# Shifting every on-chip buffer: activation tiles from 64 to 96 bytes past a 128-byte boundary

## What is computed

```python
# first block
proj = rmsnorm(x) @ w_in                       # 2048 x 6176
x = x + concat(attention, gated_linear_attention) @ w_out
h = rmsnorm(x)
x = x + (silu(h @ w_gate) * (h @ w_up)) @ w_down          # hidden width 5632
# second block
h = rms_norm(x) * (1 + sc1) + sh1              # shifts and scales from c @ w_ada
x = x + g1 * (concat(retention, rwkv, moba)(h @ w_in_2) @ w_out_2)
h = rms_norm(x) * (1 + sc2) + sh2
u = h @ w_ffn_up                               # 2048 x 11264, then a conv of width 3
x = x + g2 * ((silu(gate) * val) @ w_ffn_down)
return rms_norm(x)
```

## Time and profile before

| | us |
|---|---|
| median of 3 runs | 2443.33 |
| lowest and highest | 2442.01, 2447.37 |
| the profiled execution, span from first to last instruction | 2445.8 |
| PE busy in it | 2425.4 (99%) |
| VectorE busy | 1621.5 (66%) |
| ScalarE busy | 1149.9 (47%) |
| mean granted TensorE clock | 0.998 |

### The profile page before, as it was taken

One profiled execution on the slowest core, in us unless ns is written; L12 is line 12 of the kernel. 1 busy time (PEld: TensorE's weight loads), 2 busy tenths in 40 slices (PEclk: granted clock), 3 DMA queues, 4 the chain that ended last, 5 costly groups with the idle time before them and its releaser, 6 DMA issues.

```text
span 2445.8 us, 43133 instructions
## 1 busy us (share of the span) xinstructions
PE 2425.4 (99%) x18001; PEld 2205.9 (90%) x18001; DVE 1621.5 (66%) x1962; ACT 1149.9 (47%) x1516; POOL 0.3 (0%) x5
## 2 busy tenths in 40 slices
PE   9999999999999999999999999999999999999998
PEld 8889778999999998888899898988999999998886
DVE  5568457777777766777777455566878756664456
ACT  5465344534334334444664344445544444554444
POOL 0000000000000000000000000000000000000000
PEclk9999999999999999999999999999999999999999
DMA  8555467778777766888476344455677655555553
GB/s 280 171 170 182 150 225 268 268 263 289 275 265 285 272 238 251 317 312 293 154 279 242 125 142 139 139 185 195 245 271 258 224 207 189 190 203 193 188 187 121
DMA packets 214566, 541.27 MB, mean 221 GB/s; under 512 B 9130, under 2 KB 15860, under 8 KB 202516
## 3 DMA queue, kind: packets, MB, share of 16 engines
q1 hardware_dynamic: 214420, 539.18, 63.0%
HBM read 533.86 MB, written 5.28 MB: 220 GB/s over the span
## 4 chain that ended last, share of the span: by engine, by line
PE 97%; DVE 1%; ACT 1%; DMA 0%; issue 0%; SPq 0%; DVEq 0%; ACTq 0%
PE ps L306 36%; PE ps L1762 18%; PE ps L574 18%; PE ps L2084 15%; PE ps L1779 2%; PE ps L2602 0%; DMA raw_weights<-in_w_in_dram 0%; PE ps L2360 0%; PE ps L2621 0%; PE ps L974 0%; PE ps L1004 0%; PE ps L432 0%; PE ps L2616 0%; PE ps L986 0%; PE ps L1016 0%
## 5 line engine op out<-in xcount | busy, mean ns | idle before, releaser
L272 DVE TENSOR_TENSOR weights_lo<-raw_weights,weights_hi 128x1024 fp32r<-128x1024 f32 x786 | 957.9, 1224 | 745.4 <-ACT weights_hi L265 741.5
L265 ACT ACTIVATE weights_hi<-raw_weights 128x1024 fp32r<-128x1024 f32 x782 | 827.0, 1061 | 1182.0 <-PE ps L306 459.2
L485 DVE SCALAR_TENSOR_TENSOR ada_acc<-ada_w,col,ada_acc 128x1024 f32<-128x1024 f32 x180 | 230.1, 1278 | 0.1
L306 PE MATMUL ps<-glu_x_hi,weights_hi 128*128 128x256 f32 x1280 | 202.8, 280 | 0.0
L306 PE MATMUL ps<-glu_x_lo,weights_hi 128*128 128x256 f32 x1280 | 202.5, 279 | 0.0
L306 PE MATMUL ps<-glu_x_hi,weights_lo 128*128 128x256 f32 x1280 | 202.5, 279 | 0.0
L306 PE MATMUL ps<-conv_x_hi,weights_hi 128*128 128x256 f32 x1280 | 198.8, 277 | 0.0
L306 PE MATMUL ps<-conv_x_hi,weights_lo 128*128 128x256 f32 x1280 | 197.9, 277 | 0.0
L306 PE MATMUL ps<-conv_x_lo,weights_hi 128*128 128x256 f32 x1280 | 197.9, 277 | 0.0
L306 PEld LDWEIGHTS ps<-glu_x_lo,weights_hi 128*128 128x128 f32 x1280 | 173.2, 188 | 0.0
L306 PEld LDWEIGHTS ps<-glu_x_hi,weights_hi 128*128 128x128 f32 x1280 | 173.1, 188 | 0.0
(11 more groups left out here) (531 smaller groups left out, 3688.2 us busy)
## 6 DMA issues: line engine op xcount, KB each, us to landing
raw_weights<-in_w_in_dram SPq DMA_DIRECT2D x99, 1024.0 KB, 5.3
ada_w<-in_w_ada_dram SPq DMA_DIRECT2D x96, 1024.0 KB, 6.9
raw_weights<-in_w_ffn_up_dram SPq DMA_DIRECT2D x88, 1024.0 KB, 5.3
raw_weights<-in_w_gate_dram SPq DMA_DIRECT2D x44, 1024.0 KB, 5.1
raw_weights<-in_w_up_dram SPq DMA_DIRECT2D x44, 1024.0 KB, 5.1
raw_weights<-in_w_down_dram SPq DMA_DIRECT2D x44, 1024.0 KB, 5.4
raw_weights<-in_w_ffn_down_dram SPq DMA_DIRECT2D x44, 1024.0 KB, 4.8
raw_weights<-in_w_out_dram SPq DMA_DIRECT2D x32, 1024.0 KB, 5.1
```

The costliest lines, as they stand in the source:

```text
L265: kit.nc.scalar.activation(kit.w_hi_t[:, n % SPLITS, :], raw, ACT.Copy).then_inc(kit.w_hi, 1)
L272: kit.nc.vector.tensor_tensor(kit.w_lo_t[:, n % SPLITS, :], raw, kit.w_hi_t[:, n % SPLITS, :].bitcast(F32), ALU.subtract).then_inc(kit.w_l ...
L306: ins = nc.tensor.matmul(out, lhsT=lhsT, rhs=rhs, start=start and m == 0, stop=(k == KT - 1 and m == 2), skip_group_check=True)
L485: step = nc.vector.scalar_tensor_tensor(acc, w, c, acc, ALU.mult, ALU.add)
```

## The change

Before the first buffer a filler of 896 bytes (`head_room`) is put, so that the buffers that follow begin at a multiple of 1024: `x_rows` at 17408, `raw_weights` at 33792, `weights_hi` at 66560, `weights_lo` at 82944, `cst` at 99328. The small vectors now end at 111680, and `base` becomes the next multiple of 1024 plus 96: 112736. So

| | before | after |
|---|---|---|
| weight rings, by 128 (by 1024) | 0 (128) | 0 (0) |
| tiles placed from `base`, by 128 (by 1024) | 64 (192) | 96 (96) |
| `down_last` weights, by 128 | 64 | 96 |
| tiles in the space of `x_rows`, by 128 | 0 | 0 |
| `stat` and the vectors behind it, by 128 | 48, 64 | 48, 64 |

No instruction, wait, queue or shape changes.

```diff
+ALIGN = 1024
+SHIFT = 96
...
         sb = self.sb
+        sb("head_room", [P, (-(-nc.sbuf_base // 32) * -32 % ALIGN) // 4])
         self.x = sb("x_rows", [P, ST, D])
...
-        base = -(-nc.sbuf_base // 32) * 32
+        base = -(-nc.sbuf_base // ALIGN) * ALIGN + SHIFT
         t = lambda name, off, shape, dt=F32: kit.at_byte(name, base + off * 1024, shape, dt)
```

## The result

The changed kernel is slower. Its median is 2489.14 us (2488.79 to 2490.36 in 4 runs), beside 2445.35 us for the kernel before (2442.01 to 2447.54 in 4 runs). The ratio is 1.0184, with a 95% interval of 1.0171 to 1.0197. I had forecast 2411 us and a range up to 2464 us, so both the direction and the range were wrong.

What follows compares the result with a forecast made beforehand. The prediction took PE's large matmuls, count times pitch, to bound the kernel. T at the quick pitch throughout saved 32.1 us, all other terms 0: 2443.3 - 32.1 = 2411 us, with an 8-in-10 range of 2385 to 2464 us.

Steps and rivals of the forecast that it cites:

- What bounds the kernel: Whole kernel: PE busy 99% of the span; time is the number of large matmuls times their pitch, other engines follow.
- The counts: Large matmuls: 7,190 T matmuls at the slow pitch, 4,140 at the quick one, and 3,750 in the rows form.
- Activation tiles: PE operands' difference goes from 64 to 96; bounds 113.33 and 117.79 ns for T, 227.1 and 233.6 for rows form.
- The sum of the forecast: T matmuls at the quick pitch throughout, rows form as it was: 32.1 us less, median 2411 us; chance 0.27.
- the tail: End of the down product: rows form 227.1 ns at equal remainders, 233.0 at a difference of 64; a hint that placement matters.
- The rows form: Matmuls with weights moving: kept at the slow end, 233.6 ns, since its quick pitch was seen at equal remainders only.
- Rings: Weight rings: stay at 0 modulo 128, only the remainder by 1024 goes from 128 to 0; costed at 0.
- Rival 4: Slow T pitch everywhere, conv stretch and L574, L2084 lose: 18 us, 2462 us, chance 0.20; dearer end 74 us, 2517, 0.07 beyond.
- Wrong in another way: PE's chain: a third pitch that no row has, or PE idle with DMA as the releaser; no size given.
- Rival 3: Large matmuls: state comes from order and timing of PE's own instructions, so nothing changes; 2443 us, chance 0.17.
- Rival 2: Entry to each stretch still matters; about half the slow T matmuls change, or both forms half way: say 2426 us, chance 0.15.
- Rival 1: Rows form quick as well: 3,750 matmuls save 24 us more, 2387 us, chance 0.14.

Runs made afterwards that it cites:

- tiles0: The changed kernel with activation tiles at 0 modulo 128, equal to the weight rings at 0; 2464.99 us, 1.0080 of the kernel before.
- both96: The changed kernel with the split weights' rings also moved to 96 modulo 128, equal to the tiles; 2463.56 us, 1.0077 of the kernel before.
- the map: PE alone, layers left out: 36 matmuls in a row per pair of operand remainders, both forms; T settled at 113.3 to 120.0 ns for stationary 0.
- tiles64: The changed kernel with activation tiles back at 64 modulo 128, rings still at 0 modulo 1024; 2443.65 us, 0.9996 of the kernel before.
- entries: PE alone, layers left out: 72 T matmuls for (0, 64), (64, 0), (0, 96) after 13 preludes each; 113.3 or 117.8 ns, (0, 96) always 120.0.

## Why the prediction was wrong

**What bounds the kernel** held: PE's pitch times the count is the time, before and after, and VectorE, ScalarE and DMA follow. The counts held too (7,190 and 4,140 give 43.5 us with the measured pitches, against 42.0 by the mean gaps).

**The step that failed** is "Activation tiles", with the choice in "The sum of the forecast": "I take the quick end for T because the quick pitch already exists at this very distance and held through 3,229 matmuls, and because 32 lies nearer to the equal remainders." I carried a gain of the rows form (the tail) over to the T form, where tiles0, both96 and the map show equal remainders to be a slow place: 120.0 ns. I also counted the distance without its direction and as something to interpolate; moving 32 above the stationary operand has 116.7 ns and moving 96 has 120.0, and within 4 bytes, from 108 to 112, the pitch jumps from 120.0 to 113.3. And my bounds for T, 113.33 and 117.79 ns, were two pitches of a single pair; a pair of its own can lie outside, as this one does at 120.0. The term was -32.1 us and came out as +43.5 (by the settled pitches; +42.0 by the mean gaps). The 120.0 ns could be had from no row of before, so the upper bound should have stood well above 117.79.

**The rows form** was kept at 233.6 and measured 234.5: a term of 0 that was 3.4 us.

**Rings** at 0 us: right as far as tiles64 shows (0.9996). **Filler, VectorE, ScalarE, DMA** at 0: right by the page.

**Rival 4** had the direction and the deciding point, the pieces from 1821 us onward, but the wrong pitch: it let the slow pitch stay at 117.8 ns and came to 18 us. Its dearer end, one step more on reads off a multiple of 64, gave 74 us. The result was 43.8, and tiles0, with all T reads on multiples of 64 and as slow, showed that this is not the mechanism. The line "Wrong in another way: a third pitch that no row here has" is what happened. **Rival 3**, nothing by placement, fell with the change itself. **Rival 2** had one thing right: at distance 64 what goes before a stretch takes part in its pitch (entries). **Rival 1**'s rows-form gain exists, but at 0, 0 and 96, 96, not here.

The Trainium skill's rule that I weighed ("TensorE: Matmul & The Clock Gate", Step-by-step: what each phase is for) has two independent read ports, so that loading weights takes nothing from the running matmul. The trace doesn't bear out that places are free: with PE alone and the moving operand at 0, the T pitch was 120.0 ns with the stationary operand at 0 and 118.3 with it at 32. The Trainium skill's "SBUF — State Buffer" (Specifications (TRN2)) gives cachelines of 16 bytes and a price for each crossing into a new one. A read from any multiple of 16 crosses equally many, so by that alone such places would be alike, and in the map they are not (113.3 to 120.0 ns).

**Open:** why a pair has its pitch, and what in front of a stretch chooses between two. The experiments give a table, not a rule. I tried no tiles off a multiple of 32 in the kernel, and no kernel in which T tiles and rows tiles lie at different remainders, which the table suggests (T at distance 64, rows at 0). That an entry which differs from run to run makes the kernel before spread over 5 us, where the changed one spreads over 1.6, fits but was not shown.

## What to carry to other kernels

When PE's chain is unbroken, read the pitch (length over count) of each long piece, by form: two pitches on one line mean that something other than work sets it. The places of the two operands modulo 128 are then worth a sweep of their own, both tiles moved against each other, and each form of matmul read separately, since what is quick for one (equal remainders, 512 columns moving) is slow for another (256 columns). The pairs (64, 0) and (96, 32) beat both kernels here (by 1.1% and 1.0% against the one before), with no instruction changed. All of this is float32r with a weight load for each matmul; other formats were not tried.

## What the runs showed that I had not expected

- With PE alone and all other engines quiet, the settled T pitch goes by the operands' addresses: 113.3 to 120.0 ns at multiples of 16 bytes, up to 122.4 with places 4 bytes apart.
- Some pairs, (0, 64) and (64, 0), have two lasting pitches, 113.3 and 117.8 ns. After a single plain matmul of 48 columns both were at 117.8, after one of 80 columns both at 113.3. The pair (0, 96) has one, 120.0, after every prelude.
- Rows and T forms disagree on the best place. At equal remainders the rows form has its quickest pitch, 226.7 ns (up to 236.7 elsewhere), while the T form is at 120.0 ns (113.3 at best).
